# Starting every matmul operand at a multiple of 512 bytes in a two-layer encoder kernel

## What is computed

```python
h = h + mixer_ab(rmsnorm(h, g1), w_in, rel_a, sinks, w_out, t5_bias)   # layer 0: two kinds of attention
h = h + dense_swiglu(rmsnorm(h, g2), wg, wu, wd)                       # width 2816
h = h + mixer_c(rmsnorm(h, g1), w_in, vg, ws, bs, w_out)               # layer 1: gated positions, blocks of 128
h = h + moe_swiglu(rmsnorm(h, g2), wr, weg, weu, wed)                  # 8 experts of 3584, two for each token
return rmsnorm(h, final_norm)
```

## Time and profile before

| | us |
|---|---|
| median of three runs | 3817.87 (3813.61 to 3818.49) |
| the profiled execution | 3816.36 |
| its span, first to last instruction | 3814.7 |
| TensorE busy | 3644.6 (96%) |
| TensorE weight loads busy | 3524.1 (92%) |
| VectorE busy | 1761.4 (46%) |
| ScalarE busy | 1662.6 (44%) |
| the chain that ended last, TensorE's share | 93% |

### The profile page before, as it was taken

One profiled execution on the slowest core, in us unless ns is written; L12 is line 12 of the kernel. 1 busy time (PEld: TensorE's weight loads), 2 busy tenths in 40 slices (PEclk: granted clock), 3 DMA queues, 4 the chain that ended last, 5 costly groups with the idle time before them and its releaser, 6 DMA issues.

```text
span 3814.7 us, 76188 instructions
## 1 busy us (share of the span) xinstructions
PE 3644.6 (96%) x29176; PEld 3524.1 (92%) x29176; DVE 1761.4 (46%) x2508; ACT 1662.6 (44%) x2316; POOL 106.4 (3%) x137
## 2 busy tenths in 40 slices
PE   8999899999999999959999999999999999999993
PEld 5888799999999999749999999999999999999993
DVE  4455543333333544345555455554554444444444
ACT  3344433322332332146555465554554544544542
POOL 1000000000000000020000000000000000000001
PEclk9999999999999999979999999999999999999997
DMA  5111322223223322075655656555555445454446
GB/s 175 34 48 43 130 92 89 93 90 115 91 91 91 119 84 73 0 192 194 205 193 194 204 190 207 182 182 193 185 183 171 165 163 185 165 182 155 154 155 233
DMA packets 154482, 542.59 MB, mean 142 GB/s; under 512 B 18312, under 2 KB 18352, under 8 KB 154368
## 3 DMA queue, kind: packets, MB, share of 16 engines
q1 hardware_dynamic: 128592, 468.25, 37.6%
q0 software_dynamic: 16496, 55.52, 4.2%
q10 hardware_dynamic: 9280, 17.24, 1.5%
HBM read 511.31 MB, written 33.28 MB: 143 GB/s over the span
## 4 chain that ended last, share of the span: by engine, by line
PE 93%; DVE 2%; DMA 2%; ACT 1%; issue 1%; POOL 0%; ACTq 0%; POOLq 0%; DVEq 0%
PE ps L290 88%; PE ps L339 1%; PE ps L578 1%; PE ps L563 1%; PE ps L1522 1%; PE ps L517 1%; DMA y<-yrow_d,slot 0%; PE ps L1551 0%; PE ps L598 0%; PE ps L586 0%; PE ps L1318 0%; DMA tok_d<-tokid,slot 0%; PE ps L541 0%; ACT eA L637 0%; DMA xg<-xrow_d,tokl 0%
## 5 line engine op out<-in xcount | busy, mean ns | idle before, releaser
L277 DVE TENSOR_TENSOR wl<-wraw,wh 128x1024 fp32r<-128x1024 f32 x876 | 1071.6, 1224 | 1499.6 <-ACT wh L273 1499.0
L273 ACT ACTIVATE wh<-wraw 128x1024 fp32r<-128x1024 f32 x876 | 923.4, 1058 | 1062.3 <-PE ps L290 1054.6
L290 PE MATMUL ps<-exh,wh 128*128 128x240 f32 (+3 forms) x3584 | 1025.0, 286 | 12.2 <-issue 9.8
L290 PE MATMUL ps<-exh,wl 128*128 128x240 f32 (+3 forms) x3584 | 1025.4, 286 | 0.0
L290 PE MATMUL ps<-exl,wh 128*128 128x240 f32 (+3 forms) x3584 | 1024.4, 286 | 0.0
L290 PE MATMUL ps<-xs,wh 128*128 128x256 f32 x5248 | 848.3, 283 | 2.5 <-DVE qAl L624 2.0
L290 PEld LDWEIGHTS ps<-xs,wh 128*128 128x128 f32 x5248 | 722.6, 189 | 11.1 <-issue 7.1
L290 PEld LDWEIGHTS ps<-exh,wh 128*128 128x128 f32 x3584 | 677.6, 189 | 13.2 <-issue 13.2
L290 PEld LDWEIGHTS ps<-exl,wh 128*128 128x128 f32 x3584 | 677.2, 189 | 0.0
L290 PEld LDWEIGHTS ps<-exh,wl 128*128 128x128 f32 x3584 | 676.0, 189 | 0.0
L290 PE MATMUL ps<-xs,wl 128*128 128x256 f32 x2624 | 528.4, 283 | 0.0
(11 more groups left out here) (280 smaller groups left out, 2812.7 us busy)
## 6 DMA issues: line engine op xcount, KB each, us to landing
wraw<-in_w_expert SPq DMA_DIRECT2D x676, 512.0 KB, 3.3
wraw<-in_w_main SPq DMA_DIRECT2D x200, 512.0 KB, 3.6
yrow_d<-yst ACTq DMA_DIRECT2D x16, 512.0 KB
yT<-in_xT POOLq DMA_DIRECT2D x4, 1024.0 KB, 10.6
hT<-in_xT POOLq DMA_DIRECT2D x2, 2048.0 KB, 9.7
h_d<-hT POOLq DMA_DIRECT2D x2, 2048.0 KB, 9.7
hT<-h_d POOLq DMA_DIRECT2D x2, 2048.0 KB, 12.9
xrow_d<-rows ACTq DMA_DIRECT2D x16, 256.0 KB, 2.0
```

What stands on the lines that cost most here:

```text
L273: act.activation(wh[:, j], wraw[:, j], ACT.Copy).then_inc(hi_done, 1)
L277: dve.tensor_tensor(wl[:, j], wraw[:, j], wh[:, j].bitcast(F32), ALU.subtract).then_inc(lo_done, 1)
L290: mm = pe.matmul(out[:, s], a, b[:, s], start=first and part == 0 and c == 0, stop=last and part == 2 and c + w == n)
```

## The change

Only the order of the `sb(...)` calls, and with it the tiles' places:

```diff
+        gains = sb("gains", [P, 4, KD])
+        epsc = sb("epsc", [P, 1])
+        scope = ExitStack()
+        vstat = sb("vstat", [P, 5, NT], F32, scope)
+        scope.close()
+        gate = sb("gate", [P, 2, NT])
+        slot = sb("slot", [P, 2, NT], U32)
+        tokl = sb("tokl", [P, CAP // P], U32)
+        sb("to_512", [P, 16])
         wraw = sb("wraw", [P, 4, 1024])
         wh = sb("wh", [P, 4, 1024], F32R)
         wl = sb("wl", [P, 4, 1024], F32R)
         ident = sb("ident", [P, P])
         ones = sb("ones", [P, P])
-        gains = sb("gains", [P, 4, KD])
-        epsc = sb("epsc", [P, 1])
-        gate = sb("gate", [P, 2, NT])
-        slot = sb("slot", [P, 2, NT], U32)
-        itab = sb("itab", [1, 3, NCAND + 1], I32)
-        nitem = sb("nitem", [1, 1], I32)
-        upto = sb("upto", [1, len(WIDTHS) + 1], I32)
-        tokl = sb("tokl", [P, CAP // P], U32)
-        vstat = sb("vstat", [P, 5, NT])
...
         acc = sb("acc", [P, HALF], F32, s2)
+        itab = sb("itab", [1, 3, NCAND + 1], I32, s2)
+        nitem = sb("nitem", [1, 1], I32, s2)
+        upto = sb("upto", [1, len(WIDTHS) + 1], I32, s2)
         s2.close()
```

## The result

The changed kernel takes 3796.76 us (median of four runs, 3791.96 to 3798.97), the kernel before 3818.18 us beside it (3813.61 to 3824.08). The ratio is 0.9941, 95% interval 0.9924 to 0.9959: 0.6% or 21 us faster. Forecast were 3708 us. So the sign held and the time lies inside the stated range, but the gain is a fifth of the 110 us of the prediction's sum, and nearer to rival 1, no change.

The account below looks back on a forecast made before the run. TensorE was taken to bound the kernel, by split products times their start-to-start distance. Gains of 61.7, 26.6, 11.7, 7.5 and 2.3 us, together 110, gave 3816.4 - 110 + 2 = 3708 us; range 3640 to 3830 us.

Parts of the forecast that it names:

- the prediction's sum: Split products on L290: gains of all five column shapes, at a price per touched piece, together 110 us.
- rival 1: Split products: starts don't matter, surplus is a fixed cost of streaming while weights load; time stays 3816.4 us; chance 33%.
- What bounds the kernel: TensorE, busy 3644.6 of 3814.7 us: number of L290 products times their start-to-start distance, 120.0 ns at 256 columns.
- Where the operands start: Split products' operands: weights 128 and streamed tiles 480 bytes past a multiple of 512 before, both at 0 after.
- rival 2: Split products: two reads starting at the same place hinder each other, 2.8 ns each, 75 us slower, 3891 us; chance 17%.
- The price of a touched piece: Streamed operand of split products: each 512-byte piece touched costs about 4 ns (2.9 to 4.4 by shape); chance 50%.
- Its own test: Products of 512 columns: if the pieces are right, they gain no more than 4 ns.
- The lower bound: Gain of nothing: float32 products, transposes and kB products speak against a start's price; at best both reads together cost.
- Rivals 3 and 4: 3: eB, ptA, ptB in attention stay unaligned, 3.7 us don't come; 4: all surplus goes, towards 3547 us.
- The rule on the two read ports: Skill page: TensorE reads moving operand and weights through independent ports, never waiting; by it nothing changes.
- The size of the chances: Whole kernel: 50% a gain of a start's price, 33% rival 1, 17% rival 2.
- the likeliest case: Whole kernel: gain of a start's price, forecast 3708 us, own range 3650 to 3780 us.

Follow-up runs that it names:

- w_all64: Against a_wide: weights and all tiles behind them 64 bytes further on, so both operands start at 64 past a multiple of 512; 3734.29 us.
- w_all32: Against a_wide: weights and all tiles behind them 32 bytes further on, so both operands start at 32 past a multiple of 512; 3733.28 us.
- a_wide: Changed kernel with a token range of 512 in one product of 512 columns instead of two of 256; 3734.05 us, ratio to the kernel before 0.9784.
- p192: Changed kernel, still products of 256 columns, with all token tiles at 192 past a multiple of 512 and weights at 0; 3755.68 us, ratio to before 0.9853.
- p192_again: p192 unchanged, traced once more; 3748.06 us.
- w_m128: Against a_wide: only the streamed token tiles moved, to 128 past a multiple of 512, weights left at 0; 3769.09 us.

## Why the prediction was right or wrong

**What bounds the kernel: right.** The time is the number of split products times the distance between their starts. In every run the paces of the shapes account for the time within 5 us, and no wait took the place of a gain. The feeders had the room that was worked out, even at 3723 us, and the gain reached the end.

**Where the operands start: right in the facts, wrong in what was looked at.** The working gave both starts and then counted for each operand alone how many pieces of 512 bytes it touches. The distance, 352 or 96 modulo 256, was the quantity that mattered, and it stood only in rival 2.

**The price of a touched piece: the step that failed.** The sum was made from a surplus of 4.4, 4.4, 2.9, 3.7 and 4.0 ns a piece, read as one number. w_all64 and w_all32 refute it: both operands begin inside a piece, every product touches the additional pieces, and the paces are those of a_wide. So the cost of one piece more is nothing, within 0.2 ns; what moved the pace was the distance between the two starts. The terms came out as:

| columns | forecast, us | measured, us |
|---|---|---|
| 256 | 61.7 | 0 |
| 240 | 26.6 | 8.2 |
| 288 | 11.7 | 0 |
| 304 | 7.5 | 7.3 |
| 512 | 2.3 | 4.3 |

The term that carries the error is the 61.7 us at 256 columns. The text had the warning itself: 288 columns, with a fourth piece, have less surplus than 256 with three. A fit of five values from 2.9 to 4.4 ns was no price. That 304 columns came out as forecast is luck: the cause that gave the 7.5 us was not at work. Its own test fell too: the 512 columns were to gain no more than 4 ns, and gained 7.5.

**The lower bound: right.** The three rows that spoke for "no price of a start" (plain float32 products, transposes, products that don't stand in a steady row) were read rightly as "at best the two reads together at the full rate cost". That fits what the runs showed; it should have weighed more than the fit. The third row, the products on kB, is weak, though: it compares lengths of products, and length is not pace.

**Rival 1, a fixed cost per product: half right.** It holds for 256 and 288 columns under this change, and a_wide fits it (66 us worked out, 62.7 measured), though it doesn't prove it. It doesn't hold for 240, 304 and 512 columns, nor for 256 at distance 192.

**Rival 2, starts that coincide are slower: wrong.** Distance 0 is the fastest or level with the fastest at 288, 304 and 512 columns, and at 240 within 0.3 ns of it. The position mixing, whose operands coincide in every kernel, stayed at 111.6 ns in both kernels. At 256 columns alone distance 0 is among the slowest, and there the kernel before was no better.

**Rivals 3 and 4.** What the starts of eB, ptA and ptB cost was not measured by itself; the attention as a whole ended 2.5 us earlier. That all of the surplus goes happened in no run.

**The rule on the two read ports.** By the Trainium skill, "SBUF — State Buffer", "Who interferes with whom", nothing should have changed. The traces don't agree: the products of 512 columns take 226.7 to 234.2 ns by the relative placing of the two operands alone.

**The size of the chances.** 33% for no change and 50% for a gain of the price were set by how well the numbers fitted. A price fitted to the very surplus that it explains, with no product in the trace that lacks the cause, deserved a wider range of sizes down to zero: every value from 0 to 110 us was open, and nothing made 110 the likeliest. That the measured time lies in the range is owed to the width of the range, which reached past no change; the narrower one for the likeliest case, 3650 to 3780 us, missed it.

## What to carry to other kernels

In a steady row of reduced float32 products, TensorE's pace depended here on the shape and on the distance, modulo 256 bytes, between the starts of the streamed and the stationary operand in the partition (read in steps of 32 bytes): place them at distance 0 for 512, 304 and 288 columns, and read the pace at other shapes from a run, stage by stage. Distance 64 was as good for the whole kernel (3732.46 us against 3734.05): it lost at 512 columns what it gained at 256. Before that, make the products wide, 512 columns here: at distance 0 a product of 512 columns had no more surplus than one of 256, and that was worth 63 us where the starts alone brought 21. And judge such a change from start-to-start distances over whole stages: the mean length of a product was 282 to 286 ns in all of this, and a total mixes shapes that gained, lost and stood still.

## What the runs showed of the hardware that was not expected

- The pace is a matter of steady patterns, not of a price list. Before, products of 256 columns came 116 to 125 ns apart, in a pattern of six, after at 120 each, with the same mean of 120.0. One and the same placing ran at 113.3 or 117.8 ns for whole stages (p192, p192_again), 118.7 or 120.0 in w_m128. Inside a row that nothing interrupts the pace stayed; what sets it at the start of one stays open.
- The fastest pace seen lies at 17/16 of the column time: 226.7 ns for 512 columns, 113.3 for 256 (distance 192, or with 64 stationary columns); 240 columns came to 106.7 against 100 with 64 stationary columns, a little over it. Why it is 17/16 stays open; no steady row went below it at full clock.
- The number of stationary columns has a share in the surplus: 64 instead of 128 take 5.3 ns away at 240 columns, 6.7 at 256, 1.7 at 288 and nothing at 304.
- The operands' reads as such are not slow: plain float32 products of 512 columns (0.43 us) and the transposes (109 ns) kept their pace within 1 ns at every placing. Of the products read here, only the reduced float32 ones, with a weight load beside each, showed the effect. That the two reads meet somewhere in the memory, with a period of 256 bytes, is a guess from the table of distances and not shown.
